# Two-layer decoder trunk: the MLP weights stored in DRAM with each partition's rows of a load side by side

## The reference, cut to what matters

```python
D_MODEL, SEQ, DEPTH, D_FF = 2048, 256, 2, 8192          # batch 1, float32 throughout
def reference(x, ...):
    h = x
    for layer in range(2):
        if layer == 0: h = h + fox_mixer(rmsnorm(h, fox_norm), ...)        # forgetting attention, 16 heads of 128
        else:          h = h + retention_mixer(rmsnorm(h, ret_norm), ...)  # 8 heads, qk 256, v 512
        h = h + sqrelu_mlp(rmsnorm(h, mlp_norm[layer]), mlp_up[layer], mlp_down[layer])
    return rmsnorm(h, final_norm)

def sqrelu_mlp(h, w_up, w_down):                        # (256,2048) @ (2048,8192), then @ (8192,2048)
    return jnp.square(jax.nn.relu(h @ w_up)) @ w_down
```

## Time and profile before

| | |
|---|---|
| median of 3 runs | 2555.72 us |
| the profiled execution's own time | 2555.72 us |
| its span (first to last instruction) | 2553.9 us |
| PE / DVE / ACT busy | 2487.8 / 1963.2 / 1447.2 us |
| mean granted TensorE clock | 0.990 |
| moved by q1 / q0 | 476.65 MB / 56.12 MB |
| issue to landing, median: `in_w_stream` 512 KB | 4.5 us |
| issue to landing, median: `in_w_wide` 768 KB / 512 KB | 6.9 / 6.0 us |
| one issue on SP: `in_w_stream` / `in_w_wide` | 0.328 / 0.368 us |
| SP waits for DVE to free a place, in all | 1879 us |

### The profile page before, as it was taken

One profiled execution on the slowest core, in us unless ns is written; L12 is line 12 of the kernel. 1 busy time (PEld: TensorE's weight loads), 2 busy tenths in 40 slices (PEclk: granted clock), 3 DMA queues, 4 the chain that ended last, 5 costly groups with the idle time before them and its releaser, 6 DMA issues. The chain is left out here.

```text
span 2553.9 us, 29454 instructions
## 1 busy us (share of the span) xinstructions
PE 2487.8 (97%) x11035; PEld 2044.4 (80%) x11035; DVE 1963.2 (77%) x2007; ACT 1447.2 (57%) x1694; POOL 165.0 (6%) x284
## 2 busy tenths in 40 slices
PE   9999999999999999889999999999999999999998
PEld 8888888788788787778888888888777887877876
DVE  6454556888888888867778867777898888788887
ACT  7454544656555656545656545656565556565654
POOL 0000000000100001101111001101100010010010
PEclk9999999999999999999999999999999999999999
DMA  8454556575757575756665766657676666667574
GB/s 312 148 176 151 170 177 227 182 263 177 243 181 261 192 245 196 235 176 213 213 221 182 232 195 203 207 195 231 208 239 226 211 222 204 229 200 252 180 252 150
DMA packets 210996, 534.79 MB, mean 209 GB/s; under 512 B 17200, under 2 KB 17456, under 8 KB 210480
## 3 DMA queue, kind: packets, MB, share of 16 engines
q1 hardware_dynamic: 192832, 476.65, 55.2%
q0 software_dynamic: 17888, 56.12, 7.2%
q10 hardware_dynamic: 144, 0.26, 0.0%
HBM read 506.74 MB, written 26.21 MB: 209 GB/s over the span
## 5 line engine op out<-in xcount | busy, mean ns | idle before, releaser
L2155 DVE TENSOR_TENSOR w_lo<-work,w_hi 128x1024 fp32r<-128x1024 f32 (+2 forms) x847 | 1118.0, 1348 | 341.1 <-ACT w_hi L1533 337.8
L1533 ACT ACTIVATE w_hi<-work 128x1024 fp32r<-128x1024 f32 (+2 forms) x847 | 961.5, 1155 | 733.4 <-DMA work<-in_w_wide 191.3
L1050 PE MATMUL acc<-w_hi,xT_hi 128*128 128x512 f32 x811 | 319.0, 393 | 9.0 <-DVE xT_lo L2221 5.1
L1052 PE MATMUL acc<-w_hi,xT_lo 128*128 128x512 f32 x811 | 317.3, 391 | 0.0
L1051 PE MATMUL acc<-w_lo,xT_hi 128*128 128x512 f32 x811 | 317.2, 391 | 0.0
L1050 PE MATMUL sc<-w_hi,xT_hi 128*128 128x512 f32 x676 | 264.1, 391 | 0.0
L1052 PE MATMUL sc<-w_hi,xT_lo 128*128 128x512 f32 x676 | 263.2, 389 | 0.0
L1051 PE MATMUL sc<-w_lo,xT_hi 128*128 128x512 f32 x676 | 263.1, 389 | 0.0
L1050 PE MATMUL acc<-w_hi,aT_hi 128*128 128x512 f32 x584 | 231.5, 396 | 14.1 <-DVE h L2200 5.7
L1918 DVE TENSOR_TENSOR w_lo<-work,w_hi 128x1024 fp32r<-128x1024 f32 x127 | 151.9, 1222 | 104.1 <-ACT w_hi L1325 101.9
L1051 PE MATMUL acc<-w_lo,aT_hi 128*128 128x512 f32 x584 | 229.0, 392 | 0.0
(11 more groups left out here) (321 smaller groups left out, 3904.6 us busy)
## 6 DMA issues: line engine op xcount, KB each, us to landing
work<-in_w_stream SPq DMA_DIRECT2D x400, 512.0 KB, 4.5
work<-in_w_wide SPq DMA_DIRECT2D x212, 768.0 KB, 6.9
work<-in_w_wide SPq DMA_DIRECT2D x178, 512.0 KB, 6.0
park<-stage POOLq DMA_DIRECT2D x38, 512.0 KB, 3.2
evac<-park POOLq DMA_DIRECT2D x152, 128.0 KB, 3.8
qk_park<-evac POOLq DMA_DIRECT2D x8, 512.0 KB, 5.3
work<-qk_park POOLq DMA_DIRECT2D x32, 128.0 KB, 5.3
h<-in_x SPq DMA_DIRECT2D x2, 1024.0 KB, 8.7
```

The lines of the kernel that those rows point to most:

```text
L1050: pe.matmul(bank[:, :], x_hi, w_hi[:, c], start=start, stop=False, skip_group_check=True)
L1052: return pe.matmul(bank[:, :], x_lo, w_hi[:, c], start=False, stop=stop, skip_group_check=True)
L1533: ins = act.activation(w_hi[:, ring_cols(place, n)], src[:, first * NB:(first + n) * NB], ACT.Copy)
L2155: ins = dve.tensor_tensor(w_lo[:, c], src[:, first * NB:(first + n) * NB], w_hi[:, c].bitcast(F32), ALU.subtract)
```

## The change

In DRAM the array `w_wide` held the tiles of a load one behind another: tile, partition, column. A partition's part of a load was then two or three pieces of 2 KB, 256 KB apart. After the change the order within a load is partition, tile, column: a partition's part is one piece of 4 or 6 KB, and neighbouring partitions follow each other. The reordering is done on the host when the array is filled. Which bytes a load moves, where they land in `work`, what is waited for and the order of all instructions stay as they are.

```diff
@@ stream_of, load_units
                 flat = w_wide[unit.block + block]
-                return flat[kt * P * NB:(kt + n) * P * NB].rearrange("(k p c) -> p k c", p=P, c=NB)
+                return flat[kt * P * NB:(kt + n) * P * NB].rearrange("(p c) -> p c", p=P)
...
-                        dst = mlp_raw(u, load)
-                        if UNITS[u].kind == WIDE_PAIR:
-                            dst = dst.rearrange("p (k c) -> p k c", c=NB)
-                        sp.dma_start(dst, stream_of(u, load)).then_inc(landed[slot], 16)
+                        sp.dma_start(mlp_raw(u, load), stream_of(u, load)).then_inc(landed[slot], 16)
@@ weight_stream, put_wide
             for kts in [LEFT, RIGHT] + [range(r.kt, r.kt + r.n) for r in unit.rests if r.half == half]:
                 n = len(kts) * P * NB
-                wide[unit.block + half, at:at + n] = tiles[list(kts)].reshape(-1)
+                wide[unit.block + half, at:at + n] = tiles[list(kts)].transpose(1, 0, 2).reshape(-1)
                 at += n
```

## The result

The changed kernel takes 2564.66 us (median of 8, 2559.63 to 2571.89), the kernel before 2551.40 us (8 runs on the same chip, 2546.03 to 2559.03). The ratio is 1.0051, 95% interval 1.0034 to 1.0069. The forecast of 2550 us and the range up to 2561 us missed it. The three runs of before that were known ahead had a median 4.3 us above that of the eight, so the change itself is +13 us where -5.4 was forecast.

What follows compares the result with a forecast made beforehand. It took PE, busy 2487.8 of 2553.9 us, as the bound, with eight `mix` stalls (26.0 us) following evac's landing. Terms 0 - 2.4 - 1 - 2 = -5.4 us from 2555.72 gave 2550 us, range 2541 to 2561.

Steps and rivals of the forecast that it cites:

- What bounds the kernel: PE is nearly always busy; its eight `mix` stalls in the MLP stages, 26.0 us together, follow evac's landing.
- The packets and the lone loads: Packets of q1 fall from 192,832 to 115,776; a lone 768 KB load lands in 3.6 to 4.3 us.
- The trip at 2249 us: Round trip through DRAM by park and evac, 17.0 us before; forecast to take 16 to 17.3 us.
- (c): Start and end of a wide load: quicker with fewer pieces, -0.3 us for a round trip, between 0 and -0.9.
- (d): The eight PE stalls of `mix` in the MLP stages: 8 x -0.3 = -2.4 us, ends -12.8 and +5.6.
- Rival 3: In the round trip, park and evac get a smaller DMA share: +1.5 us each turn, 2571 us; chance 0.08.
- (b): DMA time for each byte of the wide loads: no gain from longer pieces, 0 us, ends -0.7 and +0.7 each turn.
- (e): PE's clock after the large stalls: shorter stalls bring fewer clock falls, -1 us, ends -15 and +3.4.
- (f): PE's later, small waits for `sc`, `h` and `w_lo`: loads landing sooner shorten them, -2 us, ends -8 and 0.
- Where it counted from: Starting time for the whole kernel: the profiled execution's 2555.72 us, also the median of three runs.

Runs made afterwards that it cites:

- the held ones: SP holds the prefetch until evac lands, old or changed layout, at sixteen or eight places; against the kernel before 0.9987, 0.9966, 0.9945, 0.9932.
- near_six: Kernel before, with 6 KB pieces only for the 96 three-tile loads that can queue during a contended round trip: ratio 1.0037.
- only_three: Kernel before, with the changed layout for the 212 three-tile loads alone: ratio 1.0041.
- the stretch alone: Separate kernel with only the wide loads and the DRAM round trip: trip 17.1 us beside 2 KB pieces, 19.3 us beside 6 KB.
- only_two: Kernel before, with the changed layout for the 178 two-tile loads alone (4 KB pieces): ratio 1.0006.
- far_six: Kernel before, with 6 KB pieces only for the 116 three-tile loads that meet no contended round trip: ratio 1.0010.
- the padded form: Partition order in DRAM as in the change, but 2 KB pieces 4 KB apart with zeros between; against the kernel before, ratio 1.0092.

## Why the prediction was wrong

1. *What bounds the kernel: right.* The eight stalls of `mix` follow evac's landing. All runs with clearly longer first trips wait more for `mix`, and the held ones wait about half or less. In the changed kernel the stall is ACT's wait less 1.4 to 1.9 us only if the wait for `w_lo` ahead of it is counted; the forecast's sum of 24 to 28 us for `mix` came out at 30.0, or 34.8 with `w_lo`. (Of the pairs in the prediction, 5.4 and 4.1 differ by 1.3, not by 1.4 or more.)
2. *The packets and the lone loads: right.* 115,776 packets; the lone 768 KB load took 4.2 us, within 3.6 to 4.3. The trip at 2249 us took 17.6 us, outside 16 to 17.3.
3. *The step that failed is (c) and (d), the -0.3 us for a round trip.* The forecast let the trip gain from a quicker start of the loads. First trips took +0.7 us in the changed kernel, within the scatter, and +1.2 to +1.3 in `near_six` and `only_three`; alone with five loads in flight it is +2.2 us. For (d), -2.4 us were forecast and the eight stalls grew by 4.7 us in the traces. Rival 3 named this mechanism with +1.5 for a turn and got a chance of 0.08. That its price, +12 us before the clock, is near the measured +13 is luck: the traces show +4.7 us at the eight places, not +12.
4. *Why rival 3 was held too cheap.* I set `qk_park` beside 4 KB pieces (5.3 us, a median) against park beside 2 KB (6.58 us, one contended case). The queue behind them was not equal: four slots of 512 KB there, five of 768 KB here. A fair comparison has the same backlog on both sides, and that is what the stretch alone gave: +1.6 us at 4 KB. The median itself was also a low draw: the loads of that stage are the same in all kernels, and `qk_park` reads 6.0 us on the page of the changed kernel and 5.9 to 6.4 on those of the six other kernels without a hold, for 5.3 before. The Trainium skill's rule (DMA: Bandwidth & Descriptors, "Queues, rings and completion order": engines go round the queues by the packet) pointed the right way. How much a longer piece costs does not follow from it, since a packet of that section holds several descriptors and one of the profile is a single piece: with the piece tripled, the trip grew by 13%.
5. *Term (b), no gain in rate: wrong too, with the other sign.* The rows for 2 and 4 KB came from stages with other queues. With an equal queue and no trip the long pieces take 8% less time, and q1's busy time in the kernel fell by 2%. The gain was real, but most of it landed in waits of ACT that PE does not feel.
6. *Terms (e) and (f)* hung on (d) and went with it. For (e), the clock, -1 us was forecast with +3.4 as the worse end; the granted clock fell by 0.003, up to 7.7 us by the estimate above. It fell alike in `only_three` and `near_six` (means 0.989) and not in `only_two` and `far_six` (0.991), so it goes with the long first trips. (f) can't be told from scatter in single traces. The later, small stalls did shrink in places (`sc` 5.5 to 4.3 us).
7. *Where it counted from:* 2555.72 us was a high sample of three. From 2551.4 the forecast would have been 2546.

What stays open: how much of the 8 us of the 13 that the two traces don't show is the clock and how much waits; why the DMA engines are idle for a part of the trips after the change; why 1 KB pieces did not shorten a trip in the kernel; and whether the 116 loads away from the trips cost anything (+0.10%, interval -0.02 to +0.22).

## What to carry to other kernels

Before making the pieces of a bulk transfer longer, look for a small transfer on another queue that the critical path waits for while the bulk one is queued: the bulk gets faster and the small one slower, and only one of them may count. Compare such shares at equal backlog, not by medians of different stages. When the bulk has slack, let it wait: a wait of SP ahead of a prefetch at eight places brought 0.55 to 0.68% here, more than the layout could, and with it the longer pieces are no longer a loss.

## What the runs showed of the hardware

- Beside nine 768 KB loads, five of them in flight, a 512 KB store and its read back took 15.9, 17.1, 17.6 and 19.3 us for weight pieces of 1, 2, 3 and 6 KB, and 7.9 us with nothing beside it.
- Nine 768 KB loads took 21.0 us in 2 KB pieces, 19.3 us in 6 KB and 22.1 us in 2 KB pieces 4 KB apart.
- An issue on SP took 0.328 us with one piece for a partition, 0.368 us with two to six from far apart, and 0.540 us for the padded form, where both sides have the pieces inside a partition's row.
